# Stage passages of a hybrid decoder trunk in another order: statistics, first products and early takes

## The reference

```python
s1, a1, g1, s2, a2, g2 = split(silu(c) @ ada_w[i] + ada_b[i])       # "adaLN"
x = layer_norm(ALPHA * x + g1 * mixer(x * (1 + a1) + s1), ...)
x = layer_norm(ALPHA * x + g2 * (silu(h @ wg) * (h @ wu)) @ wd, ...)  # h = x * (1 + a2) + s2
# mixer 0 (layers 0, 3): z = gelu(h @ w_in); v layer-normed, mixed over 128 positions; (u * v) @ w_out
# mixer 1 (layer 1): GLU, depthwise convolution of width 31, layer norm, silu, product with w_pw2
# mixer 2 (layer 2): latent attention, prompt and paged samples
```

## Time and profile before

| | |
|---|---|
| Three runs | 3655.67, 3664.58, 3665.48 us, median 3664.58 |
| Profiled execution | 3661.46 us, of which the span is 3659.7 |
| TensorE busy | 3249.9 us (89%) |
| VectorE busy | 1756.2 us (48%) |
| GpSimd busy | 1493.7 us (41%) |
| ScalarE busy | 481.1 us (13%) |
| Mean granted TensorE clock | 0.938 of full |
| Chain that ended last | TensorE 42%, issue 25%, GpSimd 12%, VectorE 11% |

### The profile page before, as it was taken

The page is one execution under the profiler, slowest core; times in us unless marked ns, Lnnn a source line. Parts: engine busy times, 40 slices in busy tenths (PEclk is TensorE's granted clock), DMA queues, the critical chain, the costliest instruction groups (busy, mean ns, idle before and its releaser), DMA issues.

```text
span 3659.7 us, 54461 instructions
## 1 busy us (share of the span) xinstructions
PE 3249.9 (89%) x22732; PEld 2982.0 (81%) x22732; DVE 1756.2 (48%) x2674; ACT 481.1 (13%) x1004; POOL 1493.7 (41%) x876
## 2 busy tenths in 40 slices
PE   4988789999798689999778988999987988899997
PEld 3888789999766579999775547999987988899996
DVE  2154664343667754333654446434353356643325
ACT  3110030000310130000301202100012100210001
POOL 2344335454356435454320013545542344355551
PEclk7999999999999899999887989999998999999998
DMA  5532234443211143443112112434321222122221
GB/s 191 192 102 61 73 126 136 146 124 110 71 47 41 33 149 123 144 127 97 58 39 83 37 41 104 150 122 135 125 70 48 70 80 70 52 81 82 86 79 52
DMA packets 450513, 343.82 MB, mean 94 GB/s; under 512 B 24936, under 2 KB 435936, under 8 KB 437965
## 3 DMA queue, kind: packets, MB, share of 16 engines
q1 hardware_dynamic: 443104, 333.59, 29.0%
q10 hardware_dynamic: 7165, 6.76, 0.6%
HBM read 335.77 MB, written 5.25 MB: 93 GB/s over the span
## 4 chain that ended last, share of the span: by engine, by line
PE 42%; issue 25%; POOL 12%; DVE 11%; POOLq 5%; ACT 2%; DVEq 2%; DMA 0%; ACTq 0%; SPq 0%
PE pb L722 41%; POOL w_lo L657 11%; POOLq L656 5%; DVE pb L1902 2%; DVE vn L1823 1%; DVE a_lo L1504 1%; DVE a_hi L1502 1%; ACT h_hi L1276 1%; DVE vn L1819 1%; ACT hf L1276 1%; DVE pb L1642 1%; DVE xa L1649 0%; DVEq L1822 0%; ACT xa L1289 0%; DVE xa L1647 0%
## 5 line engine op out<-in xcount | busy, mean ns | idle before, releaser
L655 POOL TENSOR_SCALAR w_hi<-w_raw 128x1024 fp32r<-128x1024 f32 (+2 forms) x416 | 440.6, 1059 | 1936.6 <-DMA w_raw<-in_gmlp_w_in 428.6
L722 PE MATMUL pb<-h_hi,w_hi 128*128 128x288 f32 x3584 | 1084.3, 303 | 83.9 <-DVE h_lo L1675 34.5
L722 PE MATMUL pb<-h_lo,w_hi 128*128 128x288 f32 x3584 | 1070.4, 299 | 0.0
L722 PE MATMUL pb<-h_hi,w_lo 128*128 128x288 f32 x3584 | 1069.2, 298 | 0.0
L657 POOL TENSOR_TENSOR w_lo<-w_raw,w_hi 128x1024 fp32r<-128x1024 f32 (+2 forms) x416 | 968.8, 2329 | 62.4 <-issue 1.7
L722 PEld LDWEIGHTS pb<-h_hi,w_hi 128*128 128x128 f32 x3584 | 688.1, 192 | 137.8 <-issue 83.3
L722 PEld LDWEIGHTS pb<-h_lo,w_hi 128*128 128x128 f32 x3584 | 687.9, 192 | 0.3
L722 PEld LDWEIGHTS pb<-h_hi,w_lo 128*128 128x128 f32 x3584 | 686.9, 192 | 0.0
L722 PE MATMUL pb<-a_hi,w_hi 128*128 128x288 f32 x2176 | 649.7, 299 | 27.1 <-DVEq L1942 11.0
L722 PE MATMUL pb<-a_hi,w_lo 128*128 128x288 f32 x2176 | 644.2, 296 | 0.0
L722 PE MATMUL pb<-a_lo,w_hi 128*128 128x288 f32 x2176 | 643.7, 296 | 0.0
(11 more groups left out here) (274 smaller groups left out, 3188.4 us busy)
## 6 DMA issues: line engine op xcount, KB each, us to landing
ada_w<-in_ada_w SPq DMA_DIRECT2D x96, 1024.0 KB, 5.7
w_raw<-in_ffn_w_gate SPq DMA_DIRECT2D x88, 512.0 KB, 4.4
w_raw<-in_ffn_w_up SPq DMA_DIRECT2D x88, 512.0 KB, 3.7
w_raw<-in_gmlp_w_in SPq DMA_DIRECT2D x64, 512.0 KB, 5.1
w_raw<-in_ffn_w_down SPq DMA_DIRECT2D x64, 512.0 KB, 3.7
w_raw<-in_gmlp_w_out SPq DMA_DIRECT2D x32, 512.0 KB, 3.7
w_raw<-in_ffn_w_down SPq DMA_DIRECT2D x32, 384.0 KB, 3.2
w_raw<-in_conv_w_pw SPq DMA_DIRECT2D x24, 512.0 KB, 3.9
```

The source lines that it names most:

```text
L655: nc.gpsimd.tensor_scalar(w_hi[:, s, 0:w], w_raw[:, s, 0:w], 1.0, 1.0, ALU.mult, ALU.mult)
L722: return nc.tensor.matmul(out, lhsT, rhs, start=start, stop=stop)
```

## The change

Five things are put in another order; the mathematics stays.

1. `down_norm` on VectorE: the first half's `Stats`, `invert` and `normalise` stand ahead of the additions of half 1, except the one of tile 4, which follows the passes of the first four tiles. `halves(0, 0)` stands ahead of the additions of tiles 5 to 7. The samples' part of an addition is added at once, per tile (in place in the bank), in place of one operation for four tiles. On TensorE the first half's statistic stands in the middle of the product of tile 4, half 1, in place of behind it.
2. `normalise` runs over tiles 0-1, 2-3 and 4-7, in place of 0-3 and 4-7, and `apply` waits per such pass.
3. TensorE takes the first four products by halves of k (`first_four`): tiles 0 to 3 for all four products, which needs only the first group of `h_ready`, then tiles 4 to 7, and the second statistic behind the first product so completed.
4. These four products are taken up early: ScalarE's part (`early`) stands between the root of half 1 and its `apply`, VectorE's part between the passes of half 1 and `samples`. `residuals` stand behind them; in the gating mixers behind product 10 of 40.
5. The adaLN pairs in a feed-forward block: four between the first and the second half of the first products (two stood behind both), then one per tile up to tile 19, in place of 21. Three of their loads are issued ahead of the block's first weights. In the convolution the state's transposes stand behind the second half's products (they stood between the halves), and the products of tile m+2 ahead of TensorE's taps of tile m, the weights being split as much earlier.

```diff
+def ada_behind(m):
+    return int(m < 20)
+def ada_used_by(n, m):
+    return min(ADA_FIRST + m - 1 + n, ADA_PAIRS)      # ADA_FIRST = 4
@@ SyncE, ffn(l)
+                    load_to(plan.mark[l, "mix"])
+                    if l == 1:
+                        sp.wait_ge(out_done, OUTS * 16)
+                    ada_to(l + 1, 3)
...
-                            ada_to(l + 1, m + 1 + n + ADA_LEAD)
+                            ada_to(l + 1, ADA1 if m == 1 else ada_used_by(n, m) + ADA_LEAD)
@@ GpSimd, conv(l)
-                    split_to(plan.mark[l, min(m + 1, KT - 1)])
+                    split_to(plan.mark[l, min(m + 2, KT - 1)])
@@ TensorE
+            def first_four(t, step, units):
+                for part_ in range(2):
+                    pe.wait_ge(h_ready, 4 * t + part_ + 1)
+                    for i in range(4):
+                        if part_ == 0:
+                            if i % 2 == 0:
+                                units(i // 2)
+                            pe.wait_ge(acc_free, G.n + i + 1)
+                        for k in range(4 * part_, 4 * part_ + 4):
+                            last = step(i, k, (G.n + i) % BANKS)
+                        if part_:
+                            last.then_inc(acc_ready, 1)
+                            if t and i == 0:
+                                second_stats()
+                G.up(4)
...
@@ TensorE, gate_up
-                    ada_pairs(2 * more)
+                    first_halves(wait_h, slots)
+                    ada_pairs(ADA_FIRST * more)
+                    for s in slots:
+                        half_product(s, KT, 1, (h_hi, h_lo), wait_h)
...
-                    ada_pairs(more)
+                    ada_pairs(more * ada_behind(first + m))
@@ TensorE, conv
-                    if 0 < m < KT - 1:
+                    if m < KT - 2:
                         s_a, s_b = take_units(2)
@@ ScalarE, apply
-            def apply(t, loads=None):
+            def apply(t, early, loads=None):
                 for h in range(2):
                     if t:
                         deviation(t, h)
+                        if h:
+                            early()
...
-                        act.wait_ge(n_ready, n + 1)
+                            if m in (0, 2, 4):
+                                act.wait_ge(n_ready, 6 * t + 3 * h + m // 2 + 1)
@@ ScalarE, gmlp
-                residuals(2 * l)
+                    if n == 10:
+                        residuals(2 * l)
@@ VectorE, down_norm
                 squares(1, 4, 7, 0, 3)
-                add_norm(e, 4, 1)
                 first = Stats(0, 5)
-                add_norm(e, 5, 1)
                 first.invert()
-                first.normalise(0)
-                add_norm(e, 6, 1)
-                first.normalise(1)
-                add_norm(e, 7, 1)
-                add_samples(4)
+                first.normalise(0, 2)
+                first.normalise(2, 4)
+                add_norm(e, 4, 1)
+                first.normalise(4, KT)
...
+                    halves(0, 0)
+                    for m in range(5, KT):
+                        add_norm(e, m, 1)
+                dve.drain().then_inc(y_ready, 1)
                 if not last:
-                    for g in range(2):
-                        halves(0, g)
+                    halves(0, 1)
                 sums(1, 4, 8, 1)
                 squares(1, 4, 8, 1, 6)
                 second = Stats(1, 7)
                 second.invert()
-                for g in range(2):
-                    second.normalise(g)
+                for m0, m1 in ((0, 2), (2, 4), (4, KT)):
+                    second.normalise(m0, m1)
                 SQ.up(7)
                 if not last:
+                    early()
                     samples(t)
                     for g in range(2):
                         halves(1, g)
```

More of the change, by code:

```diff
@@ L758, in aux_bank, with product @@
                 return BANKS + X.n % BANKS
-            def product(out, ks, w_at, m_hi, m_lo, w_moves=False):
+            def product(out, ks, w_at, m_hi, m_lo, w_moves=False, waits=None):
                 n = len(ks)
                 for q, k in enumerate(ks):
+                    if waits is not None and k % 4 == 0:
+                        pe.wait_ge(h_ready, waits + k // 4)
                     s, cols = w_at(k)
@@ L880, in down_norm @@
-                mm(sq_p, ones[:], sq[:, 7, cols], False, True).then_inc(aux_ready, 1)
+                b = acc_bank()
+                for k in range(kt):
+                    for e, (w, a) in enumerate(((w_hi, a_hi), (w_hi, a_lo), (w_lo, a_hi))):
+                        last = mm(pb[:, b, 0:HALF], w[:, slots[0], k * P:(k + 1) * P], a[:, k, half_cols(1)],
+                                  k == 0 and e == 0, k == kt - 1 and e == 2)
+                    if k == kt // 2 - 1:
+                        pe.wait_ge(part_ready, PT.n + 3)
+                        mm(mean_p, ones[:], part[:, 0, 1, cols], False, False)
+                        pe.wait_ge(y_ready, YR.n + 4)
+                        mm(mean_p, ones[:], xa[:, 7, cols], False, True).then_inc(mean_ready, 1)
+                        mm(sq_p, ones[:], part[:, 1, 1, cols], False, False)
+                        pe.wait_ge(sq_ready, SQ.n + 4)
+                        mm(sq_p, ones[:], sq[:, 7, cols], False, True).then_inc(aux_ready, 1)
@@ L1208, in _ @@
                 for n, (first, count) in enumerate(GU):
-                    gate_up(count, 2 * l + 1, n == 0, more)
+                    gate_up(first, count, 2 * l + 1, n == 0, more)
                     AR.up(2 * count)
@@ L1308, in gate, with first_gates @@
                 G.up(2)
+            def first_gates():
+                for q in range(2):
+                    gate(q, G.n % BANKS, ACT.Silu)
             def ffn_gates(count, t):
@@ L1313, in ffn_gates @@
                 if fresh:
-                    for q in range(4):
-                        gate(q % 2, G.n % BANKS, ACT.Silu)
+                    first_gates()
                     residuals(t)
@@ L1327, in conv_gate, with gmlp_v, gmlp_first @@
                 G.up(2)
+            def gmlp_v(gg, tt):
+                act.wait_ge(acc_ready, G.n + 1)
+                fn(v_sb[:, tt, gg * 256:(gg + 1) * 256], pb[:, G.n % BANKS, 0:256], ACT.Gelu).then_inc(v_ready, 1)
+                G.up()
+            def gmlp_first():
+                for n in range(4):
+                    gmlp_v(n // 2, n % 2)
             def gmlp(l):
@@ L1386, in conv @@
                     fn(sqy[:, m % 2, :], yc[:, m, :], ACT.Square).then_inc(ysq_ready, 1)
+                    if m < KT - 2:
+                        for h in range(2):
+                            conv_gate(m + 2, h)
                 act.wait_ge(st_ready, 1)
@@ L1763, in gated, with gated_split, ffn_first, gate_up @@
                                 ).then_inc(acc_free, 2)
+                G.up(2)
+            def gated_split(m, h, q):
                 dve.drain()
                 split(one(a_hi, m, half_cols(h)), one(a_lo, m, half_cols(h)), pr[:, q, :]).then_inc(a_ready, 1)
[L1766 to L1768 removed]
+            def gated(m, h, q):
+                gated_product(h, q)
+                gated_split(m, h, q)
+            def ffn_first():
+                for m in range(2):
+                    gated_product(0, m)
+            def gate_up(first, count, fresh, l):
                 more = l + 1 < DEPTH
                 if fresh:
[L1772 to L1775 removed]
+                    for m in range(2):
+                        gated_split(m, 0, m)
+                    ada_pairs(l + 1, ADA_FIRST * more)
+                    for m in range(2):
+                        gated(m, 1, m)
                 for m in range(2 * fresh, count):
@@ L1778, in gate_up, with gmlp_v, gmlp_first @@
                         gated(m, h, h)
-                    ada_pairs(l + 1, more)
+                    ada_pairs(l + 1, more * ada_behind(first + m))
+            def gmlp_v(gg, tt):
+                dve.wait_ge(v_ready, VV.up())
+                v.bn_stats(bst[:, tt, gg, :], v_sb[:, tt, gg * 256:(gg + 1) * 256]).then_inc(acc_free, 1)
+                G.up()
+            def gmlp_first():
+                for n in range(4):
+                    gmlp_v(n // 2, n % 2)
             def gmlp(l):
@@ L1915, in taps @@
                     last_.then_inc(aux_free, 1)
-                for h in range(2):
-                    for m in range(2):
-                        gated_in(m, h, m)
                 for m in range(2):
@@ L2166, in _ @@
                 for n, (first, count) in enumerate(GU):
-                    gate_up(count, n == 0, l)
+                    gate_up(first, count, n == 0, l)
                     if n < 2:
```

243 lines of the change are left out of this document (128 added, 115 removed).

## The result

The changed kernel takes 3605.22 us (median of 4 runs, 3602.99 to 3614.2) against 3665.03 of the kernel before in the same comparison: a ratio of 0.9847, 95% interval 0.9824 to 0.987. It is 1.5% faster, some 56 us. The forecast was 3585, in a range of 3560 to 3618. The profiled execution has a span of 3604.4 us (before 3659.7).

What follows compares the result with a forecast made beforehand. Passages were taken as bound by a VectorE chain, three with ScalarE's residuals behind it. Gains of 34 (feed-forward), 5 (passage 4), 20 (passage 6), 15 (passage 0) and 6.5 (passage 2) sum to 80.5 us: forecast 3585, range 3560 to 3618.

Steps and rivals of the forecast that it cites:

- First half, first product 5.0 earlier; then `h_lo` 1.4, second statistic 2.9 earlier: Passage 1, carried over to others: TensorE starts at 494.9, not 499.91; second statistic at 505.0, not 507.97.
- Statistic in mid-product, 1.1 earlier: First half of a passage: the statistic, placed in mid-product on TensorE, comes 1.1 us earlier.
- Signs: Feed-forward passages in the changed profile: first wait under 1.5 us, second 4 to 6 with 16 adaLN matmul pairs ahead.
- Second half, 13.7: Passage 1, second statistic to fifth product: 13.7 us in place of 16.7, a gain of 3.0.
- Two-tile passes, nothing: Normalising passes: no gain, as VectorE ends last though ScalarE starts 1.3 us earlier; 0.3 us added per half.
- Passage 0, 15; passage 6, 20 to the fifth product: Passage 0: 12.56 us wait plus 2.5 low clock saved; passage 6: 15.3 + 5 saved, wait falling from 22.91.
- Convolution: Passage 2 and rounds: first filtered tile 9.5 us earlier, rounds net 2 won, 5 off for low clock; 6.5 gained.
- rival of 25 us for low clock: Convolution rounds: each new 3 us wait halves the clock for 10 us, five rounds losing 5 each; 3605, chance 0.12.
- the stall's 17.5: Convolution: the 40.45 us round, stalled by GpSimd's bias ahead of needed splits, falls to 22.98, winning 17.5 us.
- Weights come late: Rival: GpSimd one 3.5 us split behind in seven passages, delaying the second statistic; 25 us lost, 3610, chance 0.10.
- Slower: Rival: slow weight loads in three feed-forward passages, each waiting some 60 us; 180 us lost, 3765, chance 0.04.
- takes late: First four products: VectorE reaches its takes while TensorE is still in them, stretching the chain; needs a 4.5 us slip.

Runs made afterwards that it cites:

- statistic behind: Changed kernel with the first half's statistics on TensorE moved back behind the whole product, not in its middle; 3593.61 us, ratio 0.9813.
- taps first: Changed kernel with TensorE's taps of tile m again ahead of the products of tile m+2, GpSimd still splitting two tiles ahead; 3589.49 us, ratio 0.98.

## Why the prediction came out as it did

- *First half, first product 5.0 earlier; then `h_lo` 1.4, second statistic 2.9 earlier.* The early start works and is worth 36 us. But I took both `h_lo` at 1.36 from the earlier trace rows, where GpSimd's last split ended at 498.01 and `h_lo` began at 498.40. Moved forward, they fell on the splits. The interval between the two statistics, forecast 1.8 shorter in each of seven passages (12.6), came out 2.3 longer in sum (173.9 for 171.6): **15 of the missing 25 us**, of which `h_lo`'s stretch is 12.6. I had weighed GpSimd only as a supplier of weights, not as a neighbour, and had read one passage only: passages 4, 6 and 7 of the same trace showed the stretch.
- *Statistic in mid-product, 1.1 earlier.* It came 0.6 earlier in passage 1 (466.75, and 467.36 when undone). Wrong in effect: undone, it gives 12 us, nearly all by who meets whom at `h_lo`.
- *Signs.* I had the first wait of a feed-forward passage under 1.5 us; it is 2.49. `h_lo`'s stretch is 1.93 of the chain ahead of it, but it is not the whole reason: with the statistic behind, where that `h_lo` takes its 1.36, the wait is still 2.15, since TensorE is through with its last product earlier (476.92 for 477.91). The second, 5.68 behind the adaLN matmuls, is in its 4 to 6.
- *Second half, 13.7.* Right: 13.93 in passage 1, 14.04 in passage 2 (981.04 - 967.0).
- *Two-tile passes, nothing.* Right for this kernel; the 0.3 us is there. It is wrong as a rule, since they gain where `h_lo` is free.
- *Passage 0, 15; passage 6, 20 to the fifth product.* Passage 0 with its mixer 17.4, of which some is luck: runs with the same code up to there took 1.7 and 4.8 us longer over it. In passage 6 the wait fell to 10.16, inside 7 to 11; 3.2 us were given back in the mixer of layer 3, in the `vn` passes (before, then after):

```profile
2785.00:3165.00 380.00, 47.38 (x56) 0.94 0.24 71
```

```profile
2729.00:3113.00 384.00, 50.55 (x56) 0.93 0.24 71
```

The passes that grew are those that scale `v_sb` into `vn`: 0.40 us each when alone, up to 2.57 when a `w_lo` of GpSimd begins within 0.1 us of them. With taps first all 56 take 47.60 us again, so this is the same meeting with GpSimd's splits, moved by a change upstream.
- *Convolution.* Up to the first filtered tile 68.4 us became 60.4, 8.0 for the 7.0 of my count. Its first half lost 3.4 where 1.4 was to be won. The five rounds, from 1027.41 to 1169.79, were to be 5 x 26.1, and 5 more for low clock; TensorE is busy in them 125.5 us, 11.2 above five times 22.87, so **the clock took 11 where 5 were counted**. The granted clock in the five was 0.86, 0.94, 0.91, 0.91 and 1.00. The rival of 25 us for low clock did not hold in full. In one round a small pass of VectorE waits as well, from its usual 0.25 us

```profile
1084.08 0.25 DVE L2037 TENSOR_SCALAR yc<-yc,par 128x64 f32<-128x64 f32 x1
...
1111.97 3.80 DVE L2037 TENSOR_SCALAR yc<-yc,par 128x64 f32<-128x64 f32 x1
```

until the GpSimd instruction beside it ends:

```profile
1111.66 4.06 POOL L695 TENSOR_TENSOR prod<-full,wdT 128x1984 f32<-128x1984 f32 x1
```

3.5 us more, in the round of 31.43. Together the stretch of rounds lost 8.7 and not 3. The experiments divide it otherwise: TensorE's order cost 16.3 where 15.5 and 5 were counted, and the split ahead won 8.5 to 10.0 where I had the stall's 17.5. So two terms of my sum were too large, one on each side, and part of the error cancelled.
- *Weights come late* happened once, in passage 0 (3.48); in passages 1 to 7 the changed kernel has no such wait. *Slower* and *takes late* did not happen.
- *Signs of being wrong.* Two of the three came in part: one round passes 30 us (31.43), and TensorE waits for `w_lo` in the middle of four products in passage 0 (3.48). The third did not: the second statistic of passage 1 is earlier, 490.87 for 507.97, though all of that was won ahead of the first.

The chain on VectorE, the full banks and the residuals were read rightly, the sign and the range too. What the prediction lacked is that VectorE's passes wait for GpSimd's instructions. The terms mis-sized were the first half (15 us), the rounds (6) and layer 3's mixer (3).

## What to carry to other kernels

When a chain is moved forward, look at what GpSimd runs at the new time: an instruction of VectorE that works in SBUF can wait for a whole GpSimd instruction (`h_lo` with two operands there, the `vn` passes with one and a result there; the passes with an operand in PSUM did not), and a duration read where it ran alone doesn't hold there. To take work a tile ahead, move the supplier (the split) and leave the consumer's order alone, unless the consumer's buffers are free that early. Small gains of one order are worth what the neighbours let through, so the parts of a change are to be undone one by one, and their combination run.

## What the hardware showed that was not expected

VectorE's `h_lo` (1.36 us alone) took up to 3.29 beside GpSimd's splits, and a pass of 64 elements 3.80 in place of 0.25; GpSimd's `w_hi` 2.15 to 2.24 in place of 1.05. In each case the second ended only after the first's instruction was over. Halving GpSimd's instruction cut that `h_lo` to 2.29 us and moved the wait to GpSimd.
